# Two-stream diffusion trunk, one core: order of the delta-gate stage, PSUM banks of the first delta tile, place of the modulation row products

## The reference

```
m = SiLU(cond) @ mod_w + mod_b        nine rows: shift, scale, gate, three times
x += 0.5 * g1 * SwiGLU_1(rms(x) * (1 + sc1) + sh1)
x += gm * [A(h) | B(h) | C(h) | D(h)] @ w_out,   h = rms(x) * (1 + scm) + shm,  one projection w_in
x += 0.5 * g2 * SwiGLU_2(rms(x) * (1 + sc2) + sh2)
```

## Time and profile before

| what | value |
|---|---|
| time, median of 3 runs | 3319.41 us (3316.92 to 3323.49) |
| time of the profiled execution | 3317.31 us |
| span of the profiled execution | 3315.6 us |
| TensorE busy | 3029.2 us (91%) |
| VectorE busy | 1463.0 us (44%) |
| ScalarE busy | 801.1 us (24%) |
| GpSimd busy | 253.5 us (8%) |
| bytes read and written by DMA | 259.00 MB, mean 78 GB/s |
| mean granted TensorE clock | 0.94 of full speed |

### The profile page before, as it was taken

The page is one execution under the profiler, slowest core; times in us unless marked ns, Lnnn a source line. Parts: engine busy times, 40 slices in busy tenths (PEclk is TensorE's granted clock), DMA queues, the critical chain, the costliest instruction groups (busy, mean ns, idle before and its releaser), DMA issues.

```text
span 3315.6 us, 58314 instructions
## 1 busy us (share of the span) xinstructions
PE 3029.2 (91%) x24855; PEld 2839.4 (86%) x24855; DVE 1463.0 (44%) x2396; ACT 801.1 (24%) x1155; POOL 253.5 (8%) x305
## 2 busy tenths in 40 slices
PE   5999999898689989999989999989976998999997
PEld 3999999895478889999989999989845887999997
DVE  3333343515556543343355444452354665444444
ACT  3221121322412231122223212222223223222221
POOL 2000000100023110000010000010001221000001
PEclk6999999998779999999999999999976899999998
DMA  7254322221000124534421222212200002122221
GB/s 240 92 174 152 128 87 76 67 62 51 2 2 4 47 92 142 177 129 136 152 77 39 76 76 76 76 64 77 74 4 3 4 3 77 55 71 69 71 76 45
DMA packets 163110, 259.00 MB, mean 78 GB/s; under 512 B 11868, under 2 KB 130884, under 8 KB 162592
## 3 DMA queue, kind: packets, MB, share of 16 engines
q1 hardware_dynamic: 140960, 174.57, 16.0%
q0 software_dynamic: 22016, 82.46, 7.4%
HBM read 253.85 MB, written 3.15 MB: 78 GB/s over the span
## 4 chain that ended last, share of the span: by engine, by line
PE 63%; issue 24%; DMA 5%; DVE 4%; ACT 1%; POOLq 1%; DVEq 1%; POOL 1%; ACTq 0%
PE ps L559 44%; PE ps L546 16%; DMA PT<-mod_w 4%; PE ps L582 1%; POOLq L436 1%; PE ps L800 1%; DMA ub<-mixer_tables 1%; DVE PT L1332 0%; DVEq L1333 0%; ACT pTs L1217 0%; DVE pexp L1573 0%; POOL dB L522 0%; PE ps L832 0%; DVE cv L1533 0%; DVE PT L1594 0%
## 5 line engine op out<-in xcount | busy, mean ns | idle before, releaser
L559 PE MATMUL ps<-hh,uh 128*128 128x320 f32 x3744 | 865.2, 313 | 58.7 <-DVE hl L1359 48.6
L559 PE MATMUL ps<-hh,ul 128*128 128x320 f32 x3744 | 858.6, 311 | 0.0
L559 PE MATMUL ps<-hl,uh 128*128 128x320 f32 x3744 | 858.5, 311 | 0.0
L559 PEld LDWEIGHTS ps<-hh,uh 128*128 128x128 f32 x3744 | 631.1, 190 | 80.8 <-issue 69.4
L559 PEld LDWEIGHTS ps<-hl,uh 128*128 128x128 f32 x3744 | 631.4, 189 | 0.0
L559 PEld LDWEIGHTS ps<-hh,ul 128*128 128x128 f32 x3744 | 631.1, 189 | 0.0
L1324 DVE TENSOR_TENSOR ul<-raw,uh 128x1024 fp32r<-128x1024 f32 x322 | 390.4, 1234 | 277.5 <-ACT uh L1040 261.7
L1369 DVE SCALAR_TENSOR_TENSOR xT<-ps,modT,xT 128x128 f32<-128x128 f32 x736 | 371.4, 547 | 302.6 <-PE ps L559 301.4
L1040 ACT CAST uh<-raw 128x1024 fp32r<-128x1024 f32 x322 | 323.7, 1046 | 486.6 <-PE ps L559 420.6
L1389 DVE SCALAR_TENSOR_TENSOR PT<-ps,PT 128x640 f32<-128x640 f32 x88 | 72.5, 824 | 771.6 <-PE ps L559 771.6
L559 PE MATMUL ps<-gh,uh 128*128 (+1 forms) x1408 | 325.0, 312 | 15.2 <-DVE ul L1324 14.3
(11 more groups left out here) (237 smaller groups left out, 2406.7 us busy)
## 6 DMA issues: line engine op xcount, KB each, us to landing
raw<-ffn_w SPq DMA_DIRECT2D x264, 512.0 KB
PT<-mod_w POOLq DMA_DIRECT2D x72, 1024.0 KB, 6.5
raw<-w_in SPq DMA_DIRECT2D x40, 512.0 KB
raw<-w_out SPq DMA_DIRECT2D x8, 768.0 KB
ub<-mixer_tables POOLq DMA_DIRECT2D x2, 2176.0 KB, 8.5
out<-PT SPq DMA_DIRECT2D x5, 512.0 KB, 2.6
PT<-x_sample SPq DMA_DIRECT2D x4, 512.0 KB, 6.0
raw<-w_out SPq DMA_DIRECT2D x16, 128.0 KB
```

The costliest lines, as they stand in the source:

```text
L559: last = pe.matmul(pair(q)[:, lo:hi], wt[:, wk * P:(wk + 1) * P], mv(mk, lo, hi), start=start and i == 0 and p_ == 0, stop=stop and i == n ...
```

## The change

In words: on PE the four key and value blocks are turned before the gate rows instead of after them. DVE no longer takes the reciprocal of the beta rows ahead of the turn: the turned columns (128 x 40) are inverted when they are copied, and the rows (8 x 640) later, after L1609 and before `gcol_ready`. In tile 0, direction 1 uses banks 2 and 3 (`next_bank`), and the two directions' steps are issued alternately. POOL's masks go in the order of the levels, and `first_turn` waits for one mask a direction, not two. The four DMAs of the context states go from POOL's queue to SP's, ahead of the load of w_out block 3. Half 0 of the modulation rows moves between the two products of `up(i, 0)`, so that half 1 comes two products of 48 matmuls after it, not one.

```diff
+        def next_bank(i, d):
+            return 0 if i else 2 * d
@@ sync, loads of w_out
+                    if j == 3:
+                        for d in range(2):
+                            sp.wait_ge(dv[d]["ose"].sem, dv[d]["ose"].at(l, 1))
+                        for h in range(2):
+                            for g in range(2):
+                                sp.dma_start(outs[4][0, l:l + 1, :, 2 * h + g].rearrange("o d k v -> (o k) d v"),
+                                             Sctx[64 * g:64 * g + 64, :, h, 64 * g:64 * g + 64]).then_inc(st_out.sem, 16)
                     sp.wait_ge(raw_free[s].sem, raw_free[s].at(l, use))
@@ gpsimd, masked
-                        if lv == 1:
+                        if lv == 0:
                             pool.wait_ge(e["lt"].sem, e["lt"].at(l, i + 1))
@@ gpsimd, tiles
-                    for lv in (1, 0, 2, 3, 4, 5):
+                    for lv in range(LEVELS):
                         masked(i, lv)
-                    if i == 1:
-                        for d in range(2):
-                            pool.wait_ge(dv[d]["ose"].sem, dv[d]["ose"].at(l, 1))
-                        settle(pool)
-                        (four dma_start of Sctx to outs[4])
@@ tensor, feed_forward
-                        up(i, 0)
                         n = i + (first - 1)
-                        pe.wait_ge(acc_used.sem, acc_used.at(l, abase + 8 * i - 8))
-                        modulation_rows(ml, 2 * n, 0)
-                        up(i, 1, lambda: modulation_rows(ml, 2 * n + 1, 1))
+
+                        def rows(half):
+                            if half == 0:
+                                pe.wait_ge(acc_used.sem, acc_used.at(l, abase + 8 * i - 8))
+                            modulation_rows(ml, 2 * n + half, half)
+                        up(i, 0, lambda: rows(0))
+                        up(i, 1, lambda: rows(1))
@@ tensor, gates
                 pe.wait_ge(pv_used.sem, pv_used.at(l, 10))
+                (the loop over the four blocks C_KC, C_KC + 1, C_VC, C_VC + 1, with its waits on kv_used)
                 pe.wait_ge(rows_ready.sem, rows_ready.at(l, 1))
...
                 mm.then_inc(gt_done.sem, 1)
-                (that loop)
@@ tensor, broadcasts and grams
-                    if d == 1:
+                    if i and d == 1:
                         pe.wait_ge(dv[0]["lt"].sem, dv[0]["lt"].at(l, i + 1))
...
-                        fp32(bank(0, P, P * h), ident[0:8, r:r + 1].to_broadcast([8, P]), gcr[:, cols])
+                        fp32(bank(z, P, P * h), ident[0:8, r:r + 1].to_broadcast([8, P]), gcr[:, cols])
                                                   (z = next_bank(i, d); bank(z + 1), bank(z + h % 2) likewise)
@@ tensor, first_turn
-                        pe.wait_ge(e["bm"].sem, e["bm"].at(l, LEVELS * i + 2))
+                        pe.wait_ge(e["bm"].sem, e["bm"].at(l, LEVELS * i + 1))
@@ vector, gates
-                ve.tensor_scalar(er, er, 1.0, None, ALU.add)
-                ve.drain()
-                ve.reciprocal(PS[0:8, :], er)
+                ve.tensor_scalar(PS[0:8, :], er, 1.0, None, ALU.add)
...
-                ve.tensor_copy(gsm[:, 0:40], bank(0, 40))
+                ve.reciprocal(gsm[:, 0:40], bank(0, 40))
...
                 ve.tensor_tensor(gk(G_BG), gk(G_BETA), gk(G_EG), ALU.mult)
+                ve.reciprocal(PS[0:8, :], PS[0:8, :])
                 ve.drain().then_inc(gcol_ready.sem, 1)
```

More of the change, by code:

```diff
@@ L818, in _ @@
                 pe.wait_ge(pv_used.sem, pv_used.at(l, 10))
+                for k, (chunk) in enumerate((C_KC, C_KC + 1, C_VC, C_VC + 1)):
+                    if k >= 2:
+                        pe.wait_ge(kv_used.sem, kv_used.at(l, k - 1))
+                    for t in range(NT):
+                        mm = pe.transpose(tiles5((4, 6)[k % 2])[:, t, :], PT[:, chunk, t * P:(t + 1) * P], ident)
+                    mm.then_inc(kv_done.sem, 1)
                 pe.wait_ge(rows_ready.sem, rows_ready.at(l, 1))
@@ L827, in _ @@
                 mm.then_inc(gt_done.sem, 1)
[L828 to L833, removed]
                 pe.wait_ge(gt_used.sem, gt_used.at(l, 1))
@@ L858, in broadcasts @@
                 def broadcasts(i, d):
-                    e, cols = dv[d], delta_tiles(i)[d]
-                    if d == 1:
+                    e, cols, z = dv[d], delta_tiles(i)[d], next_bank(i, d)
+                    if i and d == 1:
                         pe.wait_ge(dv[0]["lt"].sem, dv[0]["lt"].at(l, i + 1))
@@ L867, in broadcasts @@
                         r = 4 * d + h
[L868 removed]
+                        fp32(bank(z, P, P * h), ident[0:8, r:r + 1].to_broadcast([8, P]), gcr[:, cols])
                     for c in range(2):
                         sel = tb[0:8, T_BC + 128 * (2 * d + c):T_BC + 128 * (2 * d + c) + 128]
[L871 to L872 removed]
+                        fp32(bank(z + 1, 128, 128 * c), sel, er[:, cols])
+                        mm = fp32(bank(z + 1, 128, 256 + 128 * c), sel, PS[0:8, cols])
                     mm.then_inc(e["bcast"].sem, 1)
                 def grams(i, d):
[L877 removed]
+                    b, e, cols, z = dd[d], dv[d], delta_tiles(i)[d], next_bank(i, d)
                     pe.wait_ge(e["diff"].sem, e["diff"].at(l, i + 1))
@@ L882, in grams @@
                         kT = PT[g:g + 64, C_KC + c, cols]
-                        fp32(bank(h % 2, P, c * P), kT, PT[g:g + 64, C_QC + c, cols])
-                        mm = fp32(bank(h % 2, P, 256 + c * P), kT, b["kbT"][g:g + 64, c, :])
+                        fp32(bank(z + h % 2, P, c * P), kT, PT[g:g + 64, C_QC + c, cols])
+                        mm = fp32(bank(z + h % 2, P, 256 + c * P), kT, b["kbT"][g:g + 64, c, :])
                     mm.then_inc(e["gram"].sem, 1)
@@ L1631, in staging @@
                     for h in range(4):
-                        w = ve.scalar_tensor_tensor(b["E"][:, h, :], bank(0, P, P * h), col(G_GC, i, d, h), negm(d), ALU.subtract, ALU.min)
+                        w = ve.scalar_tensor_tensor(b["E"][:, h, :], bank(next_bank(i, d), P, P * h), col(G_GC, i, d, h), negm(d), ALU.subtract, ALU.min)
                     w.then_inc(e["diff"].sem, 1)
-                    bb = bank(1).rearrange("p (k c t) -> p k c t", k=2, c=2)
+                    bb = bank(next_bank(i, d) + 1).rearrange("p (k c t) -> p k c t", k=2, c=2)
                     ve.tensor_tensor(b["kbT"], bb[:, 1], PT[:, C_KC:C_KC + 2, cols], ALU.mult)
@@ L1641, in products @@
                     ve.wait_ge(e["gram"].sem, e["gram"].at(l, i + 1))
-                    gram = ps_all[:, 0:1024].rearrange("p (g k c t) -> p k c g t", g=2, k=2, c=2)
+                    z = 512 * next_bank(i, d)
+                    gram = ps_all[:, z:z + 1024].rearrange("p (g k c t) -> p k c g t", g=2, k=2, c=2)
                     ve.tensor_tensor(cg(b["AQ"][i % 3]), gram[:, 0], cg(b["E"]), ALU.mult)
```

3 lines of the change are left out of this document (removed).

## The result

| | before | after |
|---|---|---|
| time, median of 4 runs | 3318.16 us (3314.26 to 3323.49) | 3272.24 us (3271.25, 3271.38, 3273.09 and 10833.05) |
| profiled execution, its span | 3317.31, 3315.6 us | 3271.25, 3269.6 us |
| ratio, 95% interval | | 0.986 [0.9836, 0.9883] |

What follows compares the result with a forecast made beforehand. TensorE bounds the feed-forwards, a TensorE, VectorE and GpSimd chain the delta stage. Terms 16 + 8.5 + 20.6 + 3 = 48 us off 3317.31 give 3269, as median 3271 us; range 3256 to 3292.

Steps and rivals of the forecast that it cites:

- Modulation: Modulated feed-forward loops: half 0's earlier loads remove TensorE's 16 waits in half 1 and some low clock; 16 us.
- upper end of 22: Modulated feed-forward loops: most the moved rows could gain, 16 steps x 1.4 us = 22 us; lower end 0.
- Rival 4: Modulated feed-forward loops: modulation loads hold up the weights, eating the gain; slower, 3320 us and above; chance 3%.
- Context states: Delta stage, masks of tile 2: DMAs off POOL's queue remove TensorE's 3.66 us wait; 4.25 us a layer, 8.5 in all.
- Own banks: Delta stage, tile 0: separate banks shorten the first tile by 9.3 us a layer, its levels by 1; 20.6 us in all.
- I expect the clock to rise in the middle of the stretch: First tile: TensorE nearly without gaps, so clock rises midway; 9.3 us a layer, between 7.6 and 12.0.
- half-clock sum: First tile, broadcasts to turns' end, with the clock staying at half: 15.9 us instead of 23.46, gain 7.6.
- rival 2: First tile: clock rises early and stays up; 11.5 us there, tile 0 gains 31 us, states 10, total 3259; chance 12%.
- Gate stage: Gate stage: sum of g starts 4.0 us earlier, but the rows' reciprocal ends the stage; 1.5 us a layer, 3 in all.
- 1 fell: Modulated loops: loads share the rate and land after half 1 begins, waits stay; 3287 us; chance 18%.
- 3 by the stages: Delta stage gives back half as masks or VectorE are late, half the modulation waits stay; 3294 us; chance 5%.
- 5 by the result: Whole kernel: nothing moves on the whole; chance 2%.

Runs made afterwards that it cites:

- x1: Changed kernel with half 0 of the modulation rows put back between up(i, 0) and up(i, 1): 3288.67 us, ratio 0.9932.
- x10: Kernel before the change with only the move of half 0 of the modulation rows: 3296.22 us, ratio 0.9938.
- x5: Changed kernel with POOL's masks of level 1 ahead of level 0 again, first_turn waiting for two masks a direction: 3273.93 us, ratio 0.9873.
- x2: Changed kernel with both directions of tile 0 on banks 0 and 1 again, their steps one after the other: 3290.82 us, ratio 0.993.
- x9: Changed kernel with VectorE's gate code as before, plus 28 unread 128x128 transposes in TensorE's waits of the gate stage: 3263.35 us, ratio 0.9838.
- x6: Changed kernel with the 8 x 640 rows' reciprocal in its old place and columns only copied, TensorE's new order kept: 3268.21 us, ratio 0.9853.
- x4: Changed kernel with the old gate stage: gate rows turned first, key and value blocks behind, the rows' reciprocal ahead of the turns: 3271.10 us, ratio 0.9877.
- the control: The changed kernel run once more, unedited, beside other follow-up runs: 3271.12 us, ratio 0.9862.
- x8: Changed kernel with 15 unread 128x128 transposes on TensorE in its 3.6 us wait ahead of the first broadcasts: 3266.99 us, ratio 0.9847.

## Why the prediction was right

**Modulation, 16 us forecast.** Right in mechanism and sign. Undone it costs 17.6 us. But this is a net: the two loops alone gained 20.8 us (9.64 + 11.13), near the upper end of 22 (18.5 by x1, 17.8 by x10), and L1 FF 1 gave 4.2 back. The 1.65 us of the start do not come from this part: they stay in x1 (66.29 us) and are absent in x10 (64.42). The step was to be 47.7 to 47.9 us and is 48.14; 0.47 us above the sum of its parts stays without any wait. That the margin would hold was open in the forecast; it held, by 0.3 us in the step shown. The rule of the Trainium skill ("DMA: Bandwidth & Descriptors", section "SWDGE vs HWDGE vs iDMA"), that each DMA engine goes round-robin between its queues, fits what came: in 174 to 176 us both queues moved, 146 packets against 149, and the median landing rises from 6.4 us to 9.4. But it is the packets that are shared evenly, not the bytes: the rows got 0.54 of 0.69 MB there, not half. They began to move at 170.6 us, where the forecast had some 167, and landed at 180.48 instead of 179. Rival 4's mechanism is there too, at the size forecast (6.0 us late, at most 6 said), inside its cover of 14.

**Context states, 4.25 us a layer forecast.** Tile 1 is shorter by 5.7 and 5.6 us, and the wait of 3.66 us is gone. The price of the order of the masks, "a few tenths in tile 1 and none later", was right: x5 has the old order back and shows 0.38 us at the turns of tile 1 and none at those of tile 2. What was under-sized is the clock: at equal clock (0.95) tile 1 shrinks from 37.88 us (x10, layer 1) to 34.59, 3.3 us, less than the 4.25 taken; the other 2.3 us are the rise of the mean clock over tile 1 from 0.89 to 0.95, where 0.6 was allowed for.

**Own banks, 10.3 us a layer forecast.** The step that failed is "I expect the clock to rise in the middle of the stretch". In layer 0 it did not rise at all; in layer 1 it rose behind the grams, for the turns only. The broadcasts took 7.16 us in both, and the first tile 15.32 and 14.84 us, below the 15.9 worked out for half clock. In that sum one mask and half of the turns (0.85 + 1.0) stood behind VectorE's products; in the trace all of the turns do, 1.97 us, and the mask of direction 1 runs beside them, which is nearly the same. Of the gain, x2 gives 6.6 and 7.1 us to the banks, and x5 1.5 and 2.0 to the order of the masks. The gain is 8.2 and 8.5 us, where 9.3 was taken and 7.6 is the half-clock sum. Tile 0's levels gained 0.1 and 1.7 (1 was taken). The excess of x2's 19.7 us over these 13.7 is in stages that the edit does not reach, 2.7 us of it in the last feed-forward, and has nothing to do with banks. What the clock would have brought is seen in x9, 12.2 us for a first tile beside the 11.5 of rival 2.

**Gate stage, 1.5 us a layer forecast.** It is 1.7 and 1.1 us shorter. The sum of g starts 4.0 us earlier, as forecast, counted from the start of the stage, and the reciprocal ends the stage, as forecast; x6 shows that it takes 1.9 and 1.2 us of this away. In the total it is not to be seen: x4, with it undone, is as fast. So this term is shown in its stage and not in the time.

**Nothing in the sum for the clock elsewhere.** L1 FF 1 (-4.2), the tail of layer 1 (-6.7), the stretch ahead of its gates (+3.8) and the start (-1.65) are together 8.8 us lost in places that the change doesn't touch. The loops brought 4.8 us and tile 1 2.8 more than their terms, tiles 2 and 3 another 1.4, and that covered it, less 2.4 for the first tile, tile 0 and the gates. So the 3271 came out by terms that were off by several microseconds in both directions: that the total is right within 1 us is luck, and one execution of the same kernel differs from the next by more.

**The rivals.** 1 fell (no wait left), 2 fell by the clock, 3 by the stages (nothing is late behind the first tile that it did not count, and no modulation wait is left; masks are late for the first tile only with the old order, x5), 4 by its cover, 5 by the result.

## What to carry to other kernels

When a buffer is refilled behind its last use, the place of that use is a lever: 7 us of distance took all waits out of 16 steps, and the price, weights 6 us late, was hidden by work already queued. Where two chains take turns in one pair of PSUM banks at an idle moment, a second pair lets the two turns overlap (6.6 and 7.1 us here, of a turn of 10), but also see that the next producer in line, here POOL's masks, works in the order in which its results are needed (1.5 to 2 us). An edit of one or two microseconds in a kernel whose clock swings is to be judged by the length of its own stage; here a stage that was not edited moved by 4 to 7 us from one kernel to the next.

## What was not expected of the hardware

**The clock is not fixed by the instructions of the stage.** In L1 FF 1, TensorE comes out of an idle of the same length before the same products, before at full clock (timeline, then the stretch), and after at half:

```profile
1778.05 0.56 PE L559 MATMUL ps<-hh,uh 128*128 128x320 f32 x2 [2.48 <-ACT PT L1084]
```

```profile
1778.00:1779.00 1.00, 0.95 (x6) 1.00 0.00 0
```

The changed kernel, in the same views:

```profile
1742.09 0.90 PE L562 MATMUL ps<-hh,uh 128*128 128x320 f32 x2 [2.49 <-ACT PT L1091]
```

```profile
1742.00:1743.00 1.00, 0.91 (x3) 0.50 0.00 0
```

This restart costs 1.3 of the 4.2 us; most of the rest comes at the end of the stage, where the granted clock is lower too (0.50 over 2169 to 2173 us). Every profiled kernel with half 0 in its new place has 492 us in this stage, x10 with that edit alone too, and both kernels with the old place have 488. Why the place of half 0, in the stage before it, decides it is open. It shifts the time at which the idle falls, and x4's tail begins only 0.5 us from the changed kernel's and is 7 us shorter; but in the control everything from layer 0's mixing on came 3.5 us or more later than in the first profile of the same kernel, and every stage took the same time, the long tail and the 492 us too. So not every shift changes it. The long tail (117.2 us) came in layer 1 of the changed kernel, in both its profiles, and in layer 0 of x2, each time behind the same series of tile times (25.5, 34.6, 36.2 and 33.3 us for tiles 0 to 3): it goes with the work and the clock just ahead of it, and not with the layer.

**Busy is not enough.** The clock stayed at 0.50 over 905 to 915 us with TensorE busy throughout, and in x8 it fell from 1.00 to 0.50 between 904 and 905 us, with TensorE busy since 903.00 (behind an idle of 1.12 us), and stayed there in a stretch that was busy 5.00 of 5 us. Where the idles ahead of the stretch were filled (x9), it was up for the broadcasts, though 0.84 over the whole of 905 to 910 us.
